# A row of the expert sum on four quadrants, with TensorE's steps ahead of their evictions and six row buffers

## The reference

```python
def block(xb):                                    # 128 tokens
    q = (xb @ w_query).reshape(128, 8, 2, 128)
    sc = jnp.einsum('thpd,hpkd->thpk', q, sub_keys)
    s_top, i_top = lax.top_k(sc, 16)              # of 128, twice per head
    cand = s_top[:, :, 0, :, None] + s_top[:, :, 1, None, :]
    best, pos = lax.top_k(cand.reshape(128, 8, 256), 16)
    eidx = ...                                    # 8 x 16 expert numbers per token
    g = jax.nn.softmax(best, axis=-1)
    h = jax.nn.gelu(jnp.einsum('thkd,td->thk', expert_u[eidx], xb))
    return jnp.einsum('thk,thkd->td', g * h, expert_v[eidx])
```

## Time and profile before

| | us |
|---|---|
| median of three runs (range) | 3874.19 (3871.23 to 3879.94) |
| the profiled execution | 3888.95 |
| its span | 3887.0 |
| PE busy | 3085.5 |
| DVE busy | 1667.2 |
| ACT busy | 888.2 |
| POOL busy | 743.9 |
| rows on PE (ps<-gb,diag) | 871.6 busy, 526.9 idle before |
| gathers (gb<-in_peer_uv) | 559.8 on POOL, 1274.7 idle before |

### The profile page before, as it was taken

One profiled execution on the slowest core, in us unless ns is written; L12 is line 12 of the kernel. 1 busy time (PEld: TensorE's weight loads), 2 busy tenths in 40 slices (PEclk: granted clock), 3 DMA queues, 4 the chain that ended last, 5 costly groups with the idle time before them and its releaser, 6 DMA issues.

```text
span 3887.0 us, 38484 instructions
## 1 busy us (share of the span) xinstructions
PE 3085.5 (79%) x14550; PEld 1639.3 (42%) x14550; DVE 1667.2 (43%) x3687; ACT 888.2 (23%) x1949; POOL 743.9 (19%) x618
## 2 busy tenths in 40 slices
PE   7689988888699999999989877767776666666666
PEld 6478767626533333333347733333333222222221
DVE  3644564446410001101013355345443677676774
ACT  2223223332100000000013132343222223223221
POOL 0312412000000000000000022112222544444443
PEclk9899988779799999999998988888898878778878
DMA  3111210212599999999963478656776999999997
GB/s 116 65 52 34 74 62 1 93 59 109 221 420 420 420 420 419 419 420 420 420 273 125 176 280 300 239 217 253 279 271 256 406 420 415 419 420 419 420 419 327
DMA packets 155978, 1068.52 MB, mean 275 GB/s; under 512 B 17296, under 2 KB 19088, under 8 KB 30352
## 3 DMA queue, kind: packets, MB, share of 16 engines
q0 software_dynamic: 75408, 543.20, 35.1%
q1 hardware_dynamic: 80384, 522.87, 33.5%
HBM read 1052.63 MB, written 13.37 MB: 274 GB/s over the span
## 4 chain that ended last, share of the span: by engine, by line
PE 61%; DMA 18%; DVE 14%; ACT 5%; issue 2%; POOL 1%; ACTq 0%; DVEq 0%; SPq 0%; POOLq 0%
PE ps L92 58%; DMA gb<-in_peer_uv,eidx 16%; DVE gb L146 4%; PE ps L97 2%; DVE inv_tt L115 1%; ACT diag L168 1%; DMA ring<-in_wt 1%; ACT L168 1%; DVE wa_lo L115 1%; DVE wa_hi L130 1%; POOL gb L86 1%; DVE expert_act L115 1%; ACT dots L168 1%; DVE rw_t L134 1%; DVE prob L146 0%
## 5 line engine op out<-in xcount | busy, mean ns | idle before, releaser
L92 PE MATMUL ps<-gb,diag 64*64 64x512 f32 x4096 | 871.6, 781 | 526.9 <-ACT diag L168 515.7
L86 POOL DMA_INDIRECT gb<-in_peer_uv,eidx x512 | 559.8, 1093 | 1274.7 <-PE ps L92 980.0
L146 DVE CUSTOM_DVE_ANT_0 gb<-gb,xn 128x1024 f32<-128x1024 f32 x512 | 619.9, 1218 | 252.7 <-DMA gb<-in_peer_uv,eidx 252.4
L92 PEld LDWEIGHTS ps<-gb,diag 64*64 64x64 f32 x4096 | 273.8, 165 | 1056.6 <-ACT diag L168 781.1
L92 PE MATMUL ps<-ga,xt 128*64 128x512 f32 x1120 | 331.3, 601 | 2.5 <-DVE xt L120 2.5
L115 DVE TENSOR_TENSOR expert_act<-expert_act,ps 128x512 f32<-128x512 f32 x32 | 22.0, 687 | 542.3 <-PE ps L92 541.7
L168 ACT ACTIVATE dots<-dots 128x1 f32<-128x1 f32 (+1 forms) x346 | 70.3, 203 | 782.0 <-DVE dots L146 778.7
L115 DVE TENSOR_TENSOR x<-x,ps 128x512 f32<-128x512 f32 (+1 forms) x96 | 61.3, 642 | 418.2 <-PE ps L92 417.5
L168 ACT ACTIVATE diag<-cons,soft 128x128 f32<-128x128 f32 x512 | 205.5, 401 | 50.0 <-DVE cand L162 0.4
L92 PEld LDWEIGHTS ps<-ga,xt 128*64 128x64 f32 x1120 | 118.6, 137 | 187.9 <-issue 180.0
L92 PE MATMUL ps<-h_hi,wa_hi 128*128 128x512 f32 x368 | 159.8, 434 | 40.2 <-DVE wa_lo L115 36.2
(11 more groups left out here) (309 smaller groups left out, 4035.1 us busy)
## 6 DMA issues: line engine op xcount, KB each, us to landing
ring<-in_wt SPq DMA_DIRECT2D x77, 1024.0 KB, 5.5
ga<-in_eg SPq DMA_DIRECT2D x70, 1024.0 KB, 26.4
ga<-in_eu SPq DMA_DIRECT2D x70, 1024.0 KB, 27.0
ga<-in_ed SPq DMA_DIRECT2D x68, 1024.0 KB, 27.7
gr<-in_eu SPq DMA_DIRECT2D x37, 1024.0 KB, 27.0
gr<-in_ed SPq DMA_DIRECT2D x34, 1024.0 KB, 27.7
ring<-in_eg SPq DMA_DIRECT2D x29, 1024.0 KB, 26.4
gr<-in_eg SPq DMA_DIRECT2D x29, 1024.0 KB, 27.4
```

What stands on the lines that cost most here:

```text
L86: self.e.indirect_dma_start(out, None, table, bass.IndirectOffsetOnAxis(ap=idx, axis=0)).then_inc(s, 16)
L92: i = self.e.matmul(out, l, r, start=st, stop=sp, skip_group_check=True)
L146: self.done(self.e.tensor_tensor_reduce(out=o, in0=a, in1=b, scale=scale, scalar=start, op0=o0, op1=o1, accum_out=acc), name)
```

## The change

- PSUM: a row's first half of the columns goes to quadrants (r, r) of bank 6 and its second half to (r, 1 - r) of bank 7, in every row. The total's second half alone has to be crossed at the end of a block. The passes keep banks 0 to 5 and 6, 7 (pass 0), or 0 to 2 and 3 (pass 1, projections in the latter), and query projections and scores have banks 4 and 5.
- `m` is split: `m` is PE's part of a step of pass 1, `n` the part of ACT and DVE, one row later. In the same way `p` is followed by `q` (the eviction of a query projection, half a head later, in the second pass two rows later) and `s` (PE's scores, at step 20 of the head before) by `t` (their eviction, at step 24).
- The attention steps of the passes take half a projection in every step `u` of the first eight, not two in every second one, and the gate's parts move to later steps.
- The exponentials of a head are multiplied by 1/total in one more step of choosing (27 steps), on DVE. The weight of a row is then one ACT instruction on the column of `dots`, right after the gelu. DVE's `weight` goes.
- `w` of a group follows its own `u`; `waiting` goes.
- `XN` is split into four tiles in other places, and the passes have tiles of their own (`TN`, `gate_sq`, `gate_sp`). The room makes a sixth early buffer (`gb5`). The late rows still have thirteen.

```diff
-    EARLY = [M(f"gb{i}", 29744 + 2048 * i, 2048) for i in range(5)]
-    LATE = [T(f"gb{5 + i}", O_RING + 2048 * i, 2048) for i in range(3)] + [M(f"gb{8 + i}", 10240 + 2048 * i, 2048) for i in range(5)]
-    STEPS, GROW = 26, 180
-    VB = [4, 5, 6, 7]
+    EARLY = [M(f"gb{i}", 29744 + 2048 * i, 2048) for i in range(5)] + [M("gb5", 2048, 2048)]
+    LATE = [T(f"gb{6 + i}", O_RING + 2048 * i, 2048) for i in range(3)]
+    LATE += [M(f"gb{9 + i}", o, 2048) for i, o in enumerate((10240, 12288, 16384, 18432))]
+    STEPS, GROW = 27, 180
+    VB = [6, 7]
 
     def row_slot(n):
 
         if n < GROW:
-            return n % 5, (n - 5 if n >= 5 else None)
+            return n % 6, (n - 6 if n >= 6 else None)
...
     def peer_order():
-        yield ("p", 0, 0)
-        yield ("p", 0, 1)
-        done, p = 0, 2
-        waiting = None
+        for m in range(2):
+            yield ("p", 0, m)
+            yield ("q", 0, m)
+        yield ("s", 0, 0)
+        yield ("t", 0, 0)
+        done, p, owed = 0, 2, []
...
                 if done % 13 == 0 and p < 8:
                     yield ("p", 0, p)
+                    owed.append(("q", 0, p))
                     p += 1
-                i, h, s = done // STEPS // 8, done // STEPS % 8, done % STEPS
-                yield ("c", i, h, s)
+                if done % 13 == 6 and owed:
+                    yield owed.pop(0)
+                g, step = done // STEPS, done % STEPS
+                if step == 20 and g < 31:
+                    yield ("s", (g + 1) // 8, (g + 1) % 8)
+                if step == 24 and g < 31:
+                    yield ("t", (g + 1) // 8, (g + 1) % 8)
+                yield ("c", g // 8, g % 8, step)
                 done += 1
             for m in group:
                 yield ("u", m)
-            if waiting:
-                yield ("w", waiting)
-                if waiting[-1] % 128 == 127:
-                    yield ("out", waiting[-1] // 128)
-            if 4 <= n < 132 and n % 5 in (1, 3):
+            yield ("w", group)
+            if group[-1] % 128 == 127:
+                yield ("out", group[-1] // 128)
+            if 4 <= n < 134 and n % 5 in (0, 2):
                 yield ("m",)
-            if 132 <= n < 172 and n % 5 == 2:
-                yield ("p", 1, (n - 132) // 5)
-            waiting = group
+            if 4 <= n < 134 and n % 5 in (1, 3):
+                yield ("n",)
+            if 134 <= n < 174 and n % 5 == 4:
+                yield ("p", 1, (n - 134) // 5)
+            if 134 <= n < 174 and n % 5 == 1:
+                yield ("q", 1, (n - 136) // 5)
             n = group[-1] + 1
...
                     for half in range(2):
                         for r in range(2):
-                            to = r if k % 2 == 0 else 1 - r
-                            pe.mm(PS[VB[2 * (k % 2) + half]][64 * to:64 * to + 64, :], diag[n % 4][64 * r:64 * r + 64, 64 * r:64 * r + 64],
-                                  rows_[64 * r:64 * r + 64, 1024 + 512 * half:1536 + 512 * half], k < 2, k == 127,
+                            to = r if half == 0 else 1 - r
+                            pe.mm(PS[VB[half]][64 * to:64 * to + 64, :], diag[n % 4][64 * r:64 * r + 64, 64 * r:64 * r + 64],
+                                  rows_[64 * r:64 * r + 64, 1024 + 512 * half:1536 + 512 * half], k == 0, k == 127,
                                   ("sum", n) if half and r else None)
...
             elif ev[0] == "w":
                 for n in ev[1]:
-                    ac.wait_ge(("weight", ev[1][-1]))
+                    i, k = n // 128, n % 128
+                    d = dots[:, i % 2, k:k + 1]
+                    ac.wait_ge(("inv", i, k // 16))
+                    ac.act(d, d, ACT.Copy, scale=soft[:, i % 2, k:k + 1], name=("weight", n))
                     if n >= 4:
                         ac.wait_ge(("sum", n - 4))
-                    ac.act(diag[n % 4], ident, ACT.Copy, scale=soft[:, n // 128 % 2, n % 128:n % 128 + 1], name=("diag", n))
+                    ac.act(diag[n % 4], ident, ACT.Copy, scale=d, name=("diag", n))
...
         dv.wait_ge(("soft", i, h))
-        dv.recip(inv[:, g:g + 1], tot[:, g:g + 1], name=("inv", i, h))
+        dv.recip(inv[:, g:g + 1], tot[:, g:g + 1])
+        yield
+        e = soft[:, i % 2, 16 * h:16 * h + 16]
+        dv.ts(e, e, inv[:, g:g + 1], MUL, name=("inv", i, h))
         yield
```

In the attention steps (`pe_pass`; `ac_pass` and `dv_pass` alike):

```diff
-            if u % 2 == 0:
-                next(filler, None)
-                next(filler, None)
-            if u in (8, 9):
-                j = u - 8
+            next(filler, None)
+            if u in (12, 13):
+                j = u - 12
...
-            if u in (11, 12):
-                j = u - 11
+            if u in (15, 16):
+                j = u - 15
```

More of the change, by code:

```diff
@@ L1678, in project @@
         def project(m):
-            b, use, before = turn.next()
+            b, use, before = wide.next()
             pe.wait_ge(("tile2", TILES * p + m), ("g", p, 5), ("g", p, 7), *before)
@@ L1789, in out @@
         def out(m, dst, f, done, between=()):
-            b, use, _ = turn.next()
+            b, use, _ = wide.next()
             yield
@@ L1967, in dv_pass @@
         yield
-        turn.next()
         yield
@@ L2136, in pe_peer @@
                 s = TILES * p + P0 + m
-                b, use, before = turn.next()
+                b, use, before = few.next()
                 w = w8(ring2(s))
@@ L2143, in pe_peer @@
                               ("used", s) if a and k == 7 else None)
-            elif ev[0] == "c" and ev[3] == 0:
+            elif ev[0] == "s":
                 i, h = ev[1:3]
-                b, use, before = turn.next()
+                b, use, before = few.next()
                 pe.wait_ge(("query", i // 2, h), "sub_keys", *before)
@@ L2177, in ac_peer @@
         ac.signals("act_mix2")
-        turn = Turn("b2a", list(range(8)))
-        for _ in ac_pass(ac, 0, turn):
+        turn, wide = Turn("b2a", list(range(6))), Turn("b2r", [6, 7])
+        for _ in ac_pass(ac, 0, turn, wide):
             pass
         ac.signals("act_peer")
-        turn, _ = after_pass(turn)
-        second = ac_pass(ac, 1, turn)
+        turn, wide, few, _ = after_pass(turn, wide)
+        second, banks = ac_pass(ac, 1, turn, wide), []
         for ev in peer_order():
-            if ev[0] == "m":
+            if ev[0] == "n":
                 next(second, None)
-            elif ev[0] == "p":
+            elif ev[0] in ("p", "s"):
+                banks.append(few.next())
+            elif ev[0] == "q":
                 p, m = ev[1:]
-                b, use, _ = turn.next()
+                b, use, _ = banks.pop(0)
                 ac.wait_ge(("used", TILES * p + P0 + m))
@@ L2223, in ac_peer @@
                 ac.wait_ge(("sum", 128 * i + 127), ("dot", 128 * i + 127))
-                for half in range(2):
-                    ac.act(XN[:, i, 512 * half:512 * half + 512], PS[VB[2 + half]], ACT.Copy, name=("crossed", i))
+                ac.act(XN[i][:, 512:1024], PS[VB[1]], ACT.Copy, name=("crossed", i))
     def dv_choose(dv, i, h):
@@ L2308, in dv_peer @@
                 dv.wait_ge(("row", n), ("xn3g", i))
[L2309 to L2316 removed]
+                dv.ttr(u, u, XN[i], 1.0, 0.0, MUL, ADD, dots[:, i % 2, k:k + 1], name=("dot", n), free=True)
             elif ev[0] == "out":
```

133 lines of the change are left out of this document (55 added, 78 removed).

## The result

The changed kernel takes 3695.24 us (median of four runs, 3690.73 to 3697.52), the kernel before 3873.31 in runs beside it: a ratio of 0.9536 (95% interval 0.952 to 0.9553), 178 us or 4.6% less. The forecast was 3673. The profiled execution took 3690.73 us with a span of 3688.6.

The account below looks back on a forecast made before the run. Early rows (786 us) were taken as bound by PE, ACT and DVE taking turns, late rows by DMA. Early 197 us plus tail 4: 3888.95 - 201 = 3688, as a median 3673; range 3595 to 3768.

Parts of the forecast that it names:

- The stretch and its next bound: Early rows: DMA bounds next, 499 us at 419 GB/s; 499/0.88 plus 20 gives 587 us, 3.37 per row.
- PE-heavy cycles: Early rows, four cycles of five rows with eight half projections: about 19 us against 14.4 by DMA; adds 20 us.
- From the profiled execution to the median: Whole kernel: 201 us off the profiled 3888.95 gives 3688; its median lay 14.8 us lower, so 3673.
- Four quadrants: A row's sum on PE: halves on different quadrants overlap, a lone row takes 1.07 us instead of 1.93.
- Rival 4: PE in every row: the four quadrants don't run at once, 450 us slower, 4324; slower cases together 0.07.
- 153 us less on PE: Early rows' PE time falls from 344 to 191 us; bounds nothing saved and 172 us.
- Steps ahead: PE's steps before their evictions: removes most ACT and DVE waits for PE and PE's 211 us for diag.
- Buffers and order: Early rows: six buffers and no row held back allow 2.2 to 2.5 us per row; buffers stop being the bound.
- Weights on ScalarE: Row weight moves from DVE to ACT, 0.20 us per early row there: nothing, between -5 and +5 us.
- rival 3: Early rows: PE's clock falls; at half level throughout PE needs 760 us, 25 us won, 3849; chance 0.05.
- Head and tail: First scores some 7 us earlier, row 0's sum at 2235 against 2236.13; tail some 4 us shorter.
- Rival 2: Early rows: the turns remain, 100 to 155 us saved, pace 3.6 to 3.9, 3720 to 3774; chance 0.18.

Follow-up runs that it names:

- the last step ahead: Changed kernel with PE's step of pass 1 and the second query projections ahead of its row's sum instead of behind it: 3640.03 us, ratio 0.9388 to 0.943.

## Why the prediction was right, and where it was not

The forecast of the whole was 22 us low of a gain of 178.

- **The stretch and its next bound.** The pace was forecast at 3.37 us with a DMA share of 0.88, and is 3.38 with 0.89; row 180 was forecast at 2827 and is gathered at 2826.93. This was the step with the least behind it (the share of 0.88 was chosen between a piece of the trace and full), so its closeness is partly luck. The two shares are not even the same quantity: 499/0.88 + 20 is bytes over what 419 GB/s would move, 0.85 of it over the whole stretch, and measured that is 348/419 = 0.83; the 0.89 is the engines' busy share, which was 0.71 before at 263/419 = 0.63. Two small terms cancelled as well: row 6 went out at 2238.34 and not at 2235, and the stretch took 588.6 us and not 587 + 5. And against the second execution of the kernel before the same stretch gained 182 us, not 195.5.
- **PE-heavy cycles.** This term came out. Four cycles of five rows at 19 us, 20 us above DMA's pace in all: rows 59 to 79 took 76.7 us, 19.2 per cycle. The rows of the second query projections were put at 14 to 15 us for five and took 14.6. What the forecast had as an even loss of 12% elsewhere was not even: rows 79 to 99 took 4.1 us each, 25 us above DMA's 2.87 for the twenty, with no engine full.
- **From the profiled execution to the median.** Here the 22 us lie. The sum was made against one execution of before (3888.95 us) and its gain, 201 us, carried over whole to the median. Execution against execution the gain is 198 us, as summed. But the kernel before, profiled again, took 3861.56 us, 171 above the changed one, with its first row 16 us earlier and its stretch 13.5 us shorter; median against median it is 178. The other part is the changed kernel's profiled execution, which is the fastest of its four, 4.5 us under their median. I gave the 14.8 us between the first execution of before and its median as 0.4% and then treated them as a constant of the kernel; by the second execution such differences lie in the very stretch and head that I priced.
- **Four quadrants.** 1.07 us for a lone row; it is 1.09. The trace disagrees with the page on bank access (the Trainium skill, TensorEngine Tiling (Array Packing), section Restrictions and Gotchas) in the changed kernel too: all four quadrants of a row, with two row tiles in each of two banks, end within 1.09 us, when each record lasts 0.59 to 0.64. Rival 4 fell. Its price had a slip: 1.93/2 x 4 is 3.86 us per row and not 3.6, so its total would have been some 4455.
- **What the quadrants are worth.** PE's rows were to fall to 191 us and fell to 215: 1.23 us each where a lone one at full clock takes 1.09, so more of them ran at the half clock than I carried over from before (2.00 against 1.93). That is inferred from these times. Their saving is worth 18 us coming last and 31 coming first, and the sum never needed it: PE was not the next bound. "153 us less on PE" measured 131 (347 to 215), nearly without effect.
- **Steps ahead.** Forecast without a price of its own; it is 93 us coming last, the largest part. ACT's wait at the queries fell to 19.5 us, not quite to nothing, DVE's at prob only by half. I took one row of lead to be enough to find PE's work done. It isn't always, and the last step ahead (the step before the row's sum) brought 55 us more. The 0 to 10 us for the three banks were not measured.
- **Buffers and order.** "Buffers stop being the bound" holds: one fewer costs 16 us, the row held back 15. The round by which I argued it was not measured.
- **Weights on ScalarE.** The term was mis-sized: 0.295 us per row on ACT, not 0.20. A group of the changed kernel, 2238 to 2827, with the gelu on the same column under it:

```profile
L168 ACT ACTIVATE dots<-dots,soft 128x1 f32<-128x1 f32 x173 | 51.0, 295 | 5.6
L168 ACT ACTIVATE dots<-dots 128x1 f32<-128x1 f32 x172 | 34.9, 203 | 193.1 <-DVE dots L146 188.6
```

  The Trainium skill, ScalarE: Activation LUTs, section What ACT_TABLE_LOAD costs, gives an activation some 93 ns more for each operand that is a pointer to a column. The weight reads its scale from a column and the gelu doesn't, and the rows differ by 92 ns: the trace agrees, and I should have used it. It cost nothing that the medians show.
- **The clock.** 0.87 forecast, 0.87 found; rival 3 didn't come about in the changed kernel, and in part with the quadrants alone (0.80).
- **Head and tail.** The first scores came at 2199.27 instead of 2204.10, 4.8 us earlier and not 7. Neither can be read from one execution: in the kernel before, profiled again, they come at 2187.81, and in the changed kernel's variants with the same head between 2183.46 and 2197.70. The tail gave 0.9 us instead of 4, the last two rows' 3.49 us on the half clock instead of some 1.95.
- **Rival 2** ("the turns remain") was the nearest to be partly true. 129 us of PE's waits for the diag were left, and a change of order alone that brought them to 95 took 55 us off the end.

## What to carry to other kernels

Where engines walk through one common order, what matters is where the producer's step stands against the waits of its own queue: put work that needs nothing of the current item ahead of the instruction that waits for it, not behind. Taking work off an engine that waits for others gave little here (31 and 18 us for 153 forecast), and adding some cost little; ask which wait it ends. And compare a stretch between two events that both kernels have, since a whole execution may carry 15 us from elsewhere.

## What the runs showed of the hardware

PE's granted clock moved with the schedule, and against the saving. In the early stretch, the same work in different orders and packings: PE busy 500 of 738 us had 0.80, 488 of 698 had 0.82, 571 of 784 and 459 of 589 had 0.87, 573 of 670 had 0.94, 555 of 617 had 0.96. A PE term from a trace is a term at that trace's clock. Estimated as busy time times clock, 134 us more work (533 against 399, without the quadrants) reached the end as 18, and 97 us less (400 against 497, quadrants alone) as 31.

Four 64 x 64 quadrants of one row run side by side at full rate each, 8 records of 0.59 to 0.64 us in 1.09 us.
